# Opening of a fused recurrent/attention/MoE block on one core: weight loads issued at the start, level masks made later, three projections and convolutions moved between the weight splits

## What is computed

```
proj = rmsnorm(h) @ w_in                      # 1024 x 3080: xb, gb, q, k, v, z (512 each), b, a (4 each)
y_lru = rmsnorm(rglru(conv4(xb)) * gelu(gb))  # diagonal recurrence; gates through 8 blocks of 64 x 64
y_dn  = gated_delta(silu(conv4(q, k, v)), b, a), normed per head, * silu(z)
h = h + concat(y_lru, y_dn) @ w_out
h = h + top-1 group / top-2 expert MLPs(rmsnorm(h))   # 32 experts, 1024 -> 256 -> 1024
out = rmsnorm(h)[16:]
```

## Time and profile before

| | us |
|---|---|
| median of 3 runs | 3287.71 |
| lowest and highest | 3282.05 and 3289.16 |
| the profiled execution, its device time | 3290.71 |
| span of the profiled execution | 3289.1 |
| PE busy | 3008.6 |
| DVE busy | 2583.4 |
| ACT busy | 1996.8 |
| POOL busy | 946.8 |

### The profile page before, as it was taken

One profiled execution on the slowest core, in us unless ns is written; L12 is line 12 of the kernel. 1 busy time (PEld: TensorE's weight loads), 2 busy tenths in 40 slices (PEclk: granted clock), 3 DMA queues, 4 the chain that ended last, 5 costly groups with the idle time before them and its releaser, 6 DMA issues. The chain is left out here.

```text
span 3289.1 us, 81937 instructions
## 1 busy us (share of the span) xinstructions
PE 3008.6 (91%) x28778; PEld 2249.9 (68%) x28779; DVE 2583.4 (79%) x7206; ACT 1996.8 (61%) x4412; POOL 946.8 (29%) x994
## 2 busy tenths in 40 slices
PE   2878999999999999999999999998699999999970
PEld 2767887888888788878878887885344555554430
DVE  4868887888788788878878887886788888888755
ACT  3555566665656565666656566653576777776646
POOL 3322222221222132122213222221244444444420
PEclk9889999999999999999999999998899999999985
DMA  7110111112111212112121211115387777677749
GB/s 255 33 52 8 40 66 66 66 66 73 65 66 66 72 60 72 66 66 71 63 75 59 70 65 69 60 65 198 116 256 218 235 206 215 187 219 214 216 96 395
DMA packets 117811, 380.30 MB, mean 116 GB/s; under 512 B 18560, under 2 KB 18688, under 8 KB 105216
## 3 DMA queue, kind: packets, MB, share of 16 engines
q1 hardware_dynamic: 81440, 269.70, 22.6%
q0 software_dynamic: 29216, 89.30, 11.8%
q10 hardware_dynamic: 6848, 17.12, 1.3%
HBM read 280.05 MB, written 96.01 MB: 114 GB/s over the span
## 5 line engine op out<-in xcount | busy, mean ns | idle before, releaser
L603 PE MATMUL pj<-uT,W 128*128 128x128 f16 x15840 | 980.7, 220 | 0.0
L603 PEld LDWEIGHTS pj<-uT,W 128*128 128x128 f16 x15840 | 934.9, 98 | 46.3 <-issue 38.2
L2020 DVE SCALAR_TENSOR_TENSOR W<-W,ecol 128x512 f16<-128x512 f16 x664 | 448.1, 746 | 111.8 <-ACT W L1964 110.7
L1964 ACT ACTIVATE W<-W,ecol 128x512 f16 x664 | 415.9, 708 | 79.6 <-issue 76.1
L1928 PE MATMUL bA<-W,uT 128*128 128x512 f16 x1992 | 446.6, 381 | 5.5 <-issue 4.1
L1928 PEld LDWEIGHTS bA<-W,uT 128*128 128x128 f16 x1992 | 193.4, 98 | 229.5 <-issue 11.2
L1912 PE MATMUL pj<-W,qs 128*128 x664 | 302.8, 599 | 3.1 <-issue 2.2
L1723 POOL TENSOR_TENSOR dec<-tri,g 128x512 f32<-128x512 f32 x33 | 34.4, 1041 | 937.5 <-DVE g L1476 937.5
L937 ACT ACTIVATE ht<-ht 128x512 f32<-128x512 f32 x256 | 159.7, 625 | 93.2 <-DMA ht<-w_up 88.7
L1912 PEld LDWEIGHTS pj<-W,qs 128*128 128x128 f32 x664 | 121.5, 193 | 125.3 <-issue 124.9
L967 ACT ACTIVATE qh<-bA 128x256 f32<-128x256 f32 x198 | 76.7, 387 | 193.1 <-PE bA L703 189.3
(11 more groups left out here) (442 smaller groups left out, 6337.1 us busy)
## 6 DMA issues: line engine op xcount, KB each, us to landing
ht<-w_gate SPq DMA_DIRECT2D x128, 256.0 KB, 3.4
ht<-w_up SPq DMA_DIRECT2D x128, 256.0 KB, 3.4
W<-w_gate SPq DMA_DIRECT2D x32, 1024.0 KB, 5.0
W<-w_up SPq DMA_DIRECT2D x32, 1024.0 KB, 7.9
W<-w_down SPq DMA_DIRECT2D x32, 1024.0 KB, 12.2
x_in<-xm SPq DMA_DIRECT2D x33, 512.0 KB, 4.5
ht<-xm SPq DMA_DIRECT2D x32, 512.0 KB, 3.6
h_rows<-ht SPq DMA_DIRECT2D x32, 512.0 KB, 2.6
```

The source lines that it names most:

```text
L603: mm = pe.matmul(pj[g % 2][:, j, :], w16[:, k, w_half(w_high, COL[GROUPS[g]], 512, j * P, P)], (ul if low_u else uh)[:, k, :], start=(k == ...
L1964: nc.scalar.activation(part_of(wx[par][:, 0], k), raw[:, k], ACT.Copy, scale=ecol[par][:, k:k + 1]).then_inc(sem("wx_high"), 1)
L2020: a = nc.vector.scalar_tensor_tensor(out=part_of(wx[par][:, 1], k), in0=raw[:, k], scalar=ecol[par][:, k:k + 1], in1=part_of(wx[par][:, 0] ...
```

## The change

- SP issues all weight loads in the first block: xb, q, k, then the four block-diagonal loads (after `blocks_zero`), then v, gb, z and `w_out`. ACT neither issues nor waits for the block-diagonal loads; PE waits for them before the gate products (`bd_in`).
- The six level masks move from the first block to POOL's step -2 in the second, through `ot` in place of `kd`.
- DVE's `router_columns` and `scale_of(0)` move from step -1 to step -2, ahead of the low half of tile 0's turned x.
- With `EARLY` = 3, the projections, evacuations and convolutions of xb, q and k of tile 0 move out of P of step -1 and between the splits. On PE, the step for each g is `largest(3 + g)`, `project(g)`, then two turns, then two throughs. DVE's convolution of group g - 2 follows `low_halves(g)` for g = 2, 3, 4.
- `router_turn` uses the banks `bC`, `bT` in place of the two projection banks, and `largest` uses `bO`.
- Two semaphores are merged with others (`y_pair` into `y_sum`, `b_raw` into `lvl_step`).

```diff
@@ -322,6 +324,17 @@
                 sp.dma_start(x_in[:], xm[0:P, :]).then_inc(sem("x_in"), 16)
                 sp.dma_start(gw, w_router.rearrange("(p k) n -> p k n", k=KT)).then_inc(sem("w_rt_in"), 16)
                 load_group(sp, "xb")
+                load_group(sp, "q")
+                load_group(sp, "k")
+                sp.wait_ge(sem("blocks_zero"), 1)
+
+                for dst, src in ((wr_bd, w_r), (wi_bd, w_i)):
+                    pair = src.rearrange("(j b) c d -> b c j d", b=2)
+                    for b in range(2):
+                        sp.dma_start(dst[64 * b:64 * b + 64, :, 64 * b:64 * b + 64], pair[b]).then_inc(sem("bd_in"), 16)
+                for g in GROUPS[3:]:
+                    load_group(sp, g)
+                sp.dma_start(wo, w_out.rearrange("(k p) n -> p k n", p=P)).then_inc(sem("w_out_in"), 16)
 
             @block.scalar
             def _(act):
@@ -331,14 +344,7 @@
                                  (dt_b[:], dn_dt.partition_broadcast(P)), (rb[:], b_router.partition_broadcast(P))):
                     act.dma_start(dst, src).then_inc(sem("small_in"), 16)
                     n += 16
-                act.wait_ge(sem("blocks_zero"), 1)
-
-                for dst, src in ((wr_bd, w_r), (wi_bd, w_i)):
-                    pair = src.rearrange("(j b) c d -> b c j d", b=2)
-                    for b in range(2):
-                        act.dma_start(dst[64 * b:64 * b + 64, :, 64 * b:64 * b + 64], pair[b]).then_inc(sem("bd_in"), 16)
                 act.wait_ge(sem("small_in"), n)
-                act.wait_ge(sem("bd_in"), 64)
 
                 nc.scalar.activation(nexp_a[:], nexp_a[:], ACT.Exp).then_inc(sem("exp_a"), 1)
                 nc.scalar.activation(cl[:], lcol[:, 3, :], ACT.Abs).then_inc(sem("cl_s"), 1)
@@ -407,36 +413,8 @@
                 nc.gpsimd.tensor_copy(tri16[:], kd[:, 3, :]).then_inc(sem("p_const"), 1)
                 nc.gpsimd.tensor_copy(ones16[:], ones[:]).then_inc(sem("p_const"), 1)
                 pool.wait_ge(sem("p_const"), 6)
-                done = 6
-                rooms = [room[:, n, :] for room in (Mt, kd) for n in range(4)]
-                inner = ident[:]
-                for l in range(1, 7):
...
-        retire(keep=["idx_zeroed", "x_in", "w_xb_in", "w_rt_in"])
+        retire(keep=["idx_zeroed", "x_in", "w_rt_in", "bd_in", "w_out_in"] + sorted({LOADED[g][0] for g in GROUPS}))
-        turn_banks = ((bA, bB), (pj[0], pj[1]))
+        turn_banks = ((bA, bB), (bC, bT))
@@ -505,10 +483,6 @@
-                for g in GROUPS[1:]:
-                    load_group(sp, g)
-                sp.dma_start(wo, w_out.rearrange("(k p) n -> p k n", p=P)).then_inc(sem("w_out_in"), 16)
-
...
@@ -563,6 +537,8 @@
                     if j == 0:
                         pe.wait_ge(sem("w_out_in"), 16)
+                    if j == 1:
+                        pe.wait_ge(sem("uT_ready"), 1)
                     need(pe, sem("wo_copied"), j - 1)
                     for k in range(KT):
                         mm = pe.transpose(turn_banks[j % 2][k // 4][:, k % 4, :], wo[:, j, k:D:KT], ident[:])
@@ -579,9 +555,9 @@
-                def project(s, g, *parts):
-                    if not s.P:
+                def project(s, g, *parts, early=False):
+                    if not s.P or early != (s.i == -1 and g < EARLY):
@@ -720,16 +696,20 @@
                     mm.then_inc(sem("XU_full"), 1)
 
                 def body(s):
-                    if isinstance(s.i, int) and s.i == -1:
-                        largest(0, bT)
-                        for g in range(len(GROUPS)):
-                            largest(1 + g, bT)
-                            if g > 1:
-                                router_through(2 * g - 4)
-                                router_through(2 * g - 3)
-                            if 0 < g < 5:
-                                router_turn(2 * g - 2)
-                                router_turn(2 * g - 1)
+                    if s.i == -2:
+                        largest(0, bO)
+                    if s.i == -1:
+                        largest(1, bO)
+                        largest(2, bO)
+                        for g in range(4):
+                            largest(3 + g, bO)
+                            if g < EARLY:
+                                project(s, g, 0, 1, 2, 3, early=True)
+                            router_turn(2 * g)
+                            router_turn(2 * g + 1)
+                            router_through(2 * g)
+                            router_through(2 * g + 1)
+                        pe.wait_ge(sem("bd_in"), 64)
                     project(s, 0, 0)
                     if s.G:
 
...
@@ -937,9 +917,9 @@
                             nc.scalar.activation(ht[:, 512 * (c % 2):512 * (c % 2) + 512], ht[:, 512 * (c % 2):512 * (c % 2) + 512], ACT.Square,
                                                  accum_out=sqc[:, n, c:c + 1]).then_inc(sem("w_sq"), 1)
-                def evac(s, g, name):
-
-                    if s.P:
+                def evac(s, g, name, early=False):
+
+                    if s.P and early == (s.i == -1 and g < EARLY):
                         need(act, sem(name + "_full"), s.nP)
                         need(act, sem("halo"), 4 * s.pP - 3 + g)
                         nc.scalar.activation(ext[g][:, :, 3:3 + P], pj[g % 2][:], ACT.Copy, scale=dsc[:, g:g + 1]).then_inc(sem(name + "_evac"), 1)
@@ -969,14 +949,17 @@
                         o_high(n)
 
                 def body(s):
-                    if isinstance(s.i, int) and s.i == -1:
-                        for g in range(len(GROUPS)):
-                            high_halves(g)
-                            if 0 < g < 5:
-                                turned(2 * g - 2)
-                                turned(2 * g - 1)
-                            if g > 2:
-                                raw_squares(s, 2 * g - 6, 2 * g - 5)
+                    if s.i == -1:
+                        high_halves(0)
+                        high_halves(1)
+                        for g in range(4):
+                            high_halves(2 + g)
+                            if g < EARLY:
+                                evac(s, g, ("xb", "q", "k")[g], early=True)
+                            turned(2 * g)
+                            turned(2 * g + 1)
+                            if g:
+                                raw_squares(s, 2 * g - 2, 2 * g - 1)
                         raw_squares(s, 6, 7)
                         act.wait_ge(sem("wo_through"), KT)
                     if s.i == -2:
@@ -1158,9 +1141,9 @@
-                def conv(s, g, dst, *taps):
-                    if not s.P:
+                def conv(s, g, dst, *taps, early=False):
+                    if not s.P or early != (s.i == -1 and g < EARLY):
...
@@ -1453,14 +1436,16 @@
                         second_norm(s)
 
                 def body(s):
-                    if isinstance(s.i, int) and s.i == -1:
-
+                    if s.i == -2:
                         router_columns()
                         scale_of(0)
+                    if s.i == -1:
                         for g in range(len(GROUPS)):
                             if g + 1 < len(GROUPS):
                                 scale_of(g + 1)
                             low_halves(g)
+                            if 1 < g < 2 + EARLY:
+                                conv(s, g - 2, (xc, qs, ks)[g - 2], 0, 1, 2, 3, early=True)
                         last_columns()
                         y_gains()
                     if s.P:
@@ -1705,6 +1690,35 @@
+                def level_masks():
+
+                    done = 0
+                    rooms = [room[:, n, :] for room in (Mt, ot) for n in range(4)]
+                    inner = ident[:]
...
+                        nc.gpsimd.affine_select(out=mv, in_=ov, compare_op=ALU.is_ge, fill=0.0, base=0,
+                        nc.gpsimd.affine_select(out=mv, in_=mv, compare_op=ALU.is_ge, fill=0.0, base=b - 1,
+                        nc.gpsimd.tensor_tensor(rooms[6], m, inner, ALU.subtract).then_inc(sem("lvl_step"), 1)
+                            nc.gpsimd.tensor_copy(lvl[:, l - 1, P * q:P * q + P], rooms[6]).then_inc(sem("lvl_step"), 1)
...
@@ -1714,7 +1728,9 @@
                             nc.gpsimd.tensor_copy(wo16[:, k, w_half(True, 512 * half, 512)], o_room(n)).then_inc(sem("o_split"), 1)
 
                 def body(s):
-                    if isinstance(s.i, int) and s.i == -1:
+                    if s.i == -2:
+                        level_masks()
+                    if s.i == -1:
                         for g in range(len(GROUPS)):
                             high_copied(g)
                     if s.G:
```

More of the change, by code:

```diff
@@ L69 @@
           "v": ("w_v_in", 16), "gb": ("w_gz_in", 32), "z": ("w_gz_in", 32)}
+EARLY = 3
+MASK_STEPS = 30
 U_SCALE = 512.0
@@ L1249, in router_columns @@
                     assert done[0] == GW_SET
-                    largest(0, flat_gw, bT)
```

(28 more changed lines are left out.)

34 lines of the change are left out of this document (7 added, 27 removed).

## The result

The changed kernel took 3307.45 us, the median of six runs (3302.22 to 3312.72), and the kernel before 3288.43 in six runs on the same chip (3281.09 to 3292.63). The ratio is 1.0064, with a 95% interval of 1.0047 to 1.0081: slower, by 19 us, where 3289 was forecast (no change) and 3299 was the upper end of the range. The profiled execution has a span of 3310.7 us against 3289.1.

The account below looks back on a forecast made before the run. It took DVE's chain of scales and low halves to bound the opening. A second block 12.1 us later, added convolutions and removed waits summed to a release 1.0 us later, 149.9 against 148.94: 3289 us, range 3276 to 3299.

Parts of the forecast that it names:

- the end: Behind the splits: z waits only for POOL's last copies, starts at 143.9; DVE's release at 149.9, 1.0 us later.
- The barrier: Between first and second block: SP's load issues delay the second block's start from 24.4 to 36.5, bounds 33 and 39.
- rival 1: First block: SP's issues do not hold the barrier, second block starts near 24.4; 3276.6 us, chance 0.20.
- the large loads: SP's first block: five loads at 5.3 us each make 26.6, and `w_out` takes twice 5.3.
- the block-diagonal loads themselves: SP's first block: these small loads take 2 us, with 0.7 and 4 as bounds.
- The chain: DVE's scales and low halves, with convolutions and a stall put in, run from 40.9 to 139.4.
- The stall for `w_out`: PE's `router_turn` waiting for `w_out` inside the splits, about 7 us, goes away.
- the convolutions: Three early convolutions in DVE's splits take 7.0 us each, 21.0 together; bounds 4.65 and 9.2 each.
- the stall in scale 3: DVE waits 2 us for `largest` behind PE's early projection of xb, turns and throughs; bounds 0 to 5.
- Rival 2: Tail and opening: PE runs z at half clock, 10.7 instead of 5.34 us; 9.5 later, 3297.2 us, chance 0.18.
- Rival 3: Early convolutions: exclusive port stops them while POOL copies, 9.2 us each instead of 7.0; 3295.3 us, chance 0.12.

Follow-up runs that it names:

- e1_rxc_first: Changed kernel with tile 0's `rxc` computed on DVE ahead of the splits instead of behind them; ratio to the kernel before 1.0034.
- e3_both: Changed kernel with both edits, those of e1_rxc_first and e2_late_issue; ratio to the kernel before 0.9987.
- e7_turns_first: e3_both with the last two turns and throughs ahead of the sixth `largest` on PE, their copies ahead of ACT's sixth high halves; ratio to the kernel before 0.9988.
- e12_conv_between: e10_v_out_first with k's convolution between the last two low halves again; ratio to the kernel before 0.9980.
- e2_late_issue: Changed kernel with SP's loads of v, gb, z and `w_out` issued at the head of the second block; ratio to the kernel before 1.0024.
- e11_w_out_late: Changed kernel with only the issue of `w_out` moved to the head of the second block; ratio to the kernel before 1.0047.
- e5_loads_alone: Kernel before with only SP's weight loads all issued in the first block, block-diagonal loads still on ACT; ratio to the kernel before 1.0016.
- e9_gate_after_gb: e8_conv_last with tile 0's input gate's product moved behind gb on PE; ratio to the kernel before 0.9993.
- e8_conv_last: e7_turns_first with k's convolution moved behind the last low half; ratio to the kernel before 0.9991.
- e4_no_early: Changed kernel with `EARLY` = 0, no projections or convolutions between the splits; ratio to the kernel before 1.0052.
- e10_v_out_first: e9_gate_after_gb with ACT's evacuation of v moved ahead of the second x tile; ratio to the kernel before 0.9977.

## Why the prediction was wrong

**The step that failed** is in the part on the end: "By then PE has long done the gates, v and gb, for the 17.6 us of xb, q and k are gone from it: this is where that gain ends, at a wait for POOL." PE hadn't done them. It counted PE's work and left out what PE's work waits for: the gate product for ACT's sigmoid, ACT for `rxc`, and `rxc` for its place behind DVE's splits. POOL was done at 150.03 and z started at 164.07, 14.0 us later. e1_rxc_first shows 9.0 of these to be the wait for `rxc` with the clock that it costs. The other 5 us are PE's order itself: even without the wait it can only begin the gates behind the last turns and throughs, at 140, and e3_both still has z 5.2 us behind POOL's copies. Moving these turns alone (e7_turns_first) brought 0.7 us, since ACT's sigmoid was the next wait. Only in e12_conv_between is z released by POOL, as the prediction drew it: there the turns, the input gate's product and v's evacuation have all been moved.

**The barrier**: right in kind, 3.5 us too small. SP's issues hold it, rival 1 is refuted, and e2_late_issue and e11_w_out_late show the dependence by dose. The issue of `w_out` ended at 38.9 where 35.0 was predicted. Two terms of the sum were too small. One is the large loads: e5_loads_alone, whose SP has no block-diagonal loads, ends that issue at 35.55, where the sum without their 2 us gives 33.0. The other is the block-diagonal loads themselves: with them on SP it ends at 38.9, so they cost 3.4 and not 2. The barrier behind it took 1.1 us instead of 1.5. The stated bounds, 33 to 39, missed 40.0 by one.

**The chain**: right, to 1.8 us. From the first scale to the last low half the prediction had 139.4 - 40.9 = 98.5 us, and it took 145.4 - 45.1 = 100.3. The stall for `w_out` is gone, the convolutions took 7.2 (5.01 for the twelve and 2.0 to 2.2 for the other four) where 7.0 was predicted, and the stall in scale 3 was 1.97 against 2. The whole chain ended 6.0 us late: 3.5 for the barrier, 0.7 in the router's columns, 1.8 here. POOL's last copy was 6.1 late, and with the 14.0 behind it that makes the miss of 20.1 (release at 170.05, predicted 149.9).

**Rival 2** (the lower clock in the tail) was right that the clock matters and wrong about where. z itself ran at 5.34, warm, since PE came to it out of v and gb, and not out of a wait. The cold stretch was v, 2.5 us, behind the wait that the prediction didn't have. Where PE does come to z out of a wait of 2.3 or 3.2 us (e9_gate_after_gb, e12_conv_between), z takes 7.0. So the rival's price was too high as well: 1.7 and not 5.3, because the clock comes back within z (in e9_gate_after_gb it is at 0.50 from 142 to 144 and at 1.00 from 145). Its sum also enters the stall's rise from 2 to 5 as 3.2, where it is 3.0. The Trainium skill, "TensorE: Matmul & The Clock Gate", section "HAM oscillation", tells of a kernel whose bursts of matmuls, parted by waits for DMAs, each start at the low clock. The two z's of 7.0 behind a wait, and the z's of 5.34 without one, agree with that.

**Rival 3** (the exclusive port) asked for 9.2 us per convolution, and 7.2 was measured. The copy of 5.85 us beside low halves shows that POOL can be shut out for a long time, but DVE's convolutions are not shut out by POOL's copies in the same way. One reading on which the prediction's 7.0 and its case against this rival rest was wrong: the twelve instructions of 5.71 in the earlier trace rows did not have copies beside them all the way, since POOL's last copy ended at 128.37 and they at 129.94. In e8_conv_last POOL is busy beside nearly all of them (seven copies, then two products), and the twelve take 7.74, where they take 3.49 alone. Beside a busy POOL DVE thus goes at less than half its pace, which the prediction had too mild; that 7.0 came out near 7.2 is in part luck. The runs don't settle why the two engines hold each other up so differently.

**What the change is worth, by its parts.** All are releases of tile 0. The early loads alone cost 6.1 us (e5_loads_alone). The rest of the change without the early work costs 14.3 more (e4_no_early): 3.0 at the start of the second block, with the block-diagonal loads on SP, 2.0 in the chain and 9.2 behind it, where PE's new order of the turns is the likely cause. The early projections and convolutions gain 8.2 where nothing waits for `rxc`, and the wait for `rxc` takes 9.0. The forecast had the late start and the longer chain, and lacked all that PE does and waits for behind the sixth `largest`.

**Open.** Why e7_turns_first's ACT is so late was read off its order and not tested: moving the raw squares of the expert weights behind the gates wasn't tried. Nor was a version with `rxc` first and the late issues but without any of the early projections, nor the old order of the turns with `EARLY = 0`.

## What to carry to other kernels

When work is moved ahead of other work on an in-order engine, list every small instruction that was left behind the old place, and ask who waits for it: here 0.21 us of DVE held ACT, ACT held PE, and 9.0 us hung on it. DMA issues ahead of an all-engine barrier belong to the barrier's time as soon as the queue is full; issue there only what the stretch behind it needs first. And hold a part of a change against a kernel that has the same waits: beside the changed kernel the early projections seem to be worth nothing (0.8 us), and with the wait for `rxc` out of the way they gain 8.2.

## What the runs showed of the hardware that was not expected

- An issue of 2 MB held SP for 0.66 us twice and 10.83 us the third time, then between 2.38 and 3.79 later in the same block; four small loads (0.25 MB together) held it 9.4 us between them. The length of an issue goes here with what was issued ahead of it, not with the size of the transfer. Whether bytes or pieces ahead of it count, no run parts.
- 24 matmuls of 512 columns took 5.34 us or 7.0 by whether PE had been idle for 2.3 to 3.2 us just before. The granted clock of the stretch with z's start, in e10_v_out_first (136 to 140) and in e9_gate_after_gb (140 to 144):

```profile
136.00:140.00 4.00, 4.00 (x28) 2.46 (x26) 0.00 (x0) 2.67 (x6) 1.27 (x1) 1.00 0.02 4
```

```profile
140.00:144.00 4.00, 2.43 (x6) 0.89 (x7) 0.00 (x0) 3.95 (x7) 1.27 (x1) 0.69 0.02 4
```

- One POOL copy of 512 columns took 5.85 us beside DVE's low halves back to back, and 0.61 to 0.67 beside a convolution (e8_conv_last), so a denser DVE chain can starve POOL: in e10_v_out_first, where the first of these copies took 5.85 us too, gb waited 8.15 us for POOL, and 3.46 in e12_conv_between with the convolution between.
- The second block started 1.36 us behind SP's last issue in e2_late_issue, e3_both and e11_w_out_late, whose issues ended at 23.72, 23.60 and 33.62. It is the issues that hold the barrier and not the landings: in e5_loads_alone `w_out` landed 24.8 us after 31.89, and the second block had started at 36.95.
